# Reordered mixers in layers 3 and 4, and modulation units issued inside the attention of a four-layer fp32 kernel

## The chip, the cores and the metric

The program runs on one core of a Trainium2 chip. The metric is device time in microseconds of one execution, median of several. TensorE (PE) multiplies, VectorE (DVE) and ScalarE (ACT) do elementwise work, GpSimd (POOL) does a little, SyncE (SP) issues the DMAs.

## The reference, cut to what matters

Four transformer-like layers run one after the other on 256 tokens of x and 256 context tokens, 1024 channels, all in float32. Layers 0 and 1 are "first" layers: an attention with grouped keys, a pooling branch and a Fourier branch, one output projection, then a gated feed-forward of width 2816. Layers 2 and 3 ("mixers 3 and 4") are "second" layers: eight heads of differential attention, a convolution branch with 31 taps, both gated and added, an output projection, then a feed-forward of width 4096. Layers 0 and 2 compute both streams (512 columns), layers 1 and 3 compute only x after the keys and values (256 columns).

```python
# each layer: six modulation vectors per stream, from w_ada (1024 x 6144)
mx = silu_c @ w_ada[i] + b_ada[i]        # shift1, scale1, gate1, shift2, scale2, gate2
# second layers
z = a * sigmoid(g)                        # 512 channels of px
z = conv31(z) + b_dw                      # depthwise, along the tokens
y_conv = silu(layernorm(z, ln_g, ln_b)) @ w_conv_out
w = softmax(q1 k1) - lam * softmax(q2 k2) # per head
attn = rmsnorm(w @ v) ; y_attn = attn @ w_attn_out
y = (sigmoid(g_conv) * y_conv + sigmoid(g_attn) * y_attn) @ w_out
x = x + gate1 * y
x = x + gate2 * (relu(modulate(rmsnorm(x)) @ w1) ** 2 @ w2)
```

## The kernel before, in words

Activations lie with channels on the partitions. `plan()` writes one list of steps by hand; `build()` walks that list once per engine, so every engine runs its share of the steps strictly in the list's order, and semaphores tie the engines together. What the list says is the order of everything.

**A weight block** (step `wb`, L134) is a 1024x128 piece of a weight matrix. SP loads it into one of four raw buffers (L980), ACT casts it to `w_hi` (L1157), DVE subtracts to get `w_lo` (L1391), and PE makes 24 matmuls of it, three for each of eight k-tiles (L1036, L1037, L1038), into one of two PSUM banks `out0`, `out1`. Then ACT or DVE evicts the bank. Blocks are split three ahead (AHEAD). The products of the convolution branch have only four k-tiles.

**A modulation unit** (step `ada`, L297) is a 128x1024 piece of `w_ada`. It takes a raw buffer too, all of the same size (512 KB), and PE uses it directly, with a stationary operand of two columns: four matmuls on four column groups of the array, which are eight records in the trace (L1016). Sixteen units fill one bank of modulation vectors, three banks make one layer, 192 units in all. After the sixteenth, DVE transposes the PSUM bank (L1438) and makes the vectors; the first unit of the next bank waits for that. Before, units accumulate in the score bank `sc0` or, in the second layers, in `pt1`.

**The ring of raw buffers.** Weight blocks and units form one stream in the order of the steps (blocks three steps early). SP issues entry r when entry r-4 has been used by PE (a unit) or split by DVE (a block).

**Attention items** (`attend`, L260). One item is 128 queries of one head (or of two paired heads in first layers). On PE: scores S (L1101), transposes T of the previous item's probabilities (L1111), then fill work, PV of the previous item (L1123), then more fill work. DVE takes the maximum (L1596) and normalizes (L1615), ACT makes the exponentials (L1297) and copies the transposes (L1306). Fill work are the projections of the next head, the norms, and in first layers the Fourier and pooling steps. Layer 0 has 16 items, layer 1 has 8, layer 2 has 4 in each of 8 heads, layer 3 has 2 in each of 8.

**Where units stand before.** Bank 0 of layer 0 is the opening. Banks 1 and 2 of layer 0 (32 units) stand between the 13 steps of the head of layer 0 (`spread(head[2:], ada_head)`, L529), which is everything between the first norm and the first score. Layer 1's 48 units: 8 in the second norm of layer 0, 40 spread over the feed-forward of layer 0. Layer 2's 48: 8 and 40 in the same places of layer 1. Layer 3's: 40 in the heads 0 to 3 of layer 2's attention (ten a head, `ada_left`, L717), 8 in its second norm.

**Second layers before** (`layer_second`, L556). First the four pairs of convolution blocks (gate `w_cg`, value `w_ca`), each followed by 8 taps. Then the projections, norms and turns of head 0 with 4 taps after each of their eight functions, and 3 more inside two of them. A tap is one DVE instruction over one of four 128-channel tiles (L1650, and L1647 for the first); there are 124 in a layer. 70 of them stand ahead of the first score of head 0; heads 0 to 4 get the rest. The layer norm of the convolution stands in head 4 (`conv_mean` to `conv_scale`), and its result is written to k-tiles 4 to 7 of `mix_hi`/`mix_lo`, so that the eight gated products (`gated_conv`: a block of `w_gt` and one of `w_conv_out`) have to be through, in head 5, before the output norm of head 4 may be written there. After head 7 come the output norm of head 7 (`out_norm`, L679), eight more gates and eight `w_attn_out` blocks, the merge, and `w_out2`.

Of the kernel before, what the change touches and what calls it, by code (L numbers as in the profile page):

```python
# [19 lines left out]
P = 128  # L20
F32 = mybir.dt.float32
# [75 lines left out]
def plan():  # L97
# [37 lines left out]
    def wb(layer, mat, m, src, k0, nk, n, role, **kw):  # L135
# [3 lines left out]
        s.src_ready = after("act_ready" if src == "act" else "mix_ready")  # L139
# [120 lines left out]
    def attend(items, fills):  # L260
# [4 lines left out]
        for j, item in enumerate(items):  # L265
# [31 lines left out]
    def ada(layer, bank, half, k, psum="sc"):  # L297
        s = step("ada", layer=layer, bank=bank, half=half, k=k, psum=psum)
        s.used = signal("ada_used")
        raw.append(("ada", s))  # L300
        if (half, k) == (0, 0):
            s.sc_free = last.get(("sc", 0)) if psum == "sc" else last.get(("pt", 1))
        if (half, k) == (1, KD - 1):
            s.mods = signal("mods_read")
            last[("sc", 0) if psum == "sc" else ("pt", 1)] = s.mods
            signal("mods_ready")
        return s

# [111 lines left out]
    def layer_first(layer, ada_head=(), gap=(), r=None):  # L420
# [108 lines left out]
        spread(head[2:], ada_head)  # L529
# [6 lines left out]
        for t in range(4):  # L536
# [7 lines left out]
            attend(its, rest)  # L544
        attend_last()
        last["kT", 0] = after("scores_done")
# [6 lines left out]
    def layer_second(layer, ada_head=(), first=(), gap=()):  # L553
# [9 lines left out]
        def conv_taps(count):  # L563

            todo = []
            for _ in range(count):
                t = min(range(len(glu)), key=lambda t: (taps_done[t], t))
                if taps_done[t] == CONV_K:
                    break
                before_it = tap_value[t]  # L570
# [42 lines left out]
        def conv_scale():  # L613
# [6 lines left out]
            finish_mix(s, 4)  # L620
            last["y", 0] = s.mix
# [6 lines left out]
        def product(g, mat, m, k0, nk, role):  # L628
            y = wb(layer, mat, m, "mix", k0, nk, n, role, other=g)
# [35 lines left out]
        def out_norm(h):  # L665
# [11 lines left out]
            def scale():  # L677
# [5 lines left out]
                s.mix_free = None if h < 4 else ("wb_done", state["yconv_end"])  # L683
# [8 lines left out]

        def gated_conv(m):
# [1154 lines left out]
```

## Time and profile before

| | us |
|---|---|
| median of 3 runs | 2612.6 (2610.18 to 2618.47) |
| the profiled execution, its time | 2616.48 |
| the profiled execution, its span | 2614.7 |
| PE busy in it | 2367.3 |
| DVE busy | 1389.5 |
| ACT busy | 1069.2 |
| POOL busy | 33.4 |

The mean granted TensorE clock of that execution is 0.945 of full speed, and 335.87 MB were moved, 128 GB/s on average. Two views are used most. One gives the busy time of each engine in a chosen stretch, with the clock and the DMA rate, one stretch a row. The other lists instructions in order of time, with the idle time ahead of each in square brackets and what ended it. The stretches are cut where the list of steps has its joints: the first score matmul of a head, the first block of a matrix.

### The profile page before, as it was taken

How to read it: one execution, taken by the hardware profiler on the slowest of the kernel's cores; microseconds unless marked ns; L12 is line 12 of the kernel's file. 1: busy time of each engine (PE TensorE's matmuls, PEld its weight loads, DVE VectorE, ACT ScalarE, POOL GpSimd, SP SyncE). 2: the span in 40 equal slices, each digit the busy share in tenths (PEclk: the TensorE clock that was granted, in tenths of full speed). 3: DMA queues.
4: the chain of work that ended last, by engine and by line, in shares of the span. 5: the costliest groups of instructions: out<-in, count | busy, mean ns of one | idle time of the engine just before them, and what ended most of it. 6: DMA issues, size and time to landing. Idle time of an engine off the chain costs nothing.

```text
span 2614.7 us, 34654 instructions
## 1 busy us (share of the span) xinstructions
PE 2367.3 (91%) x13646; PEld 1878.6 (72%) x13646; DVE 1389.5 (53%) x2341; ACT 1069.2 (41%) x1838; POOL 33.4 (1%) x40
## 2 busy tenths in 40 slices
PE   5798899999888999879979899899999788988999
PEld 2466677777666888656658677588888666868999
DVE  4154423333565444788763534544345887555665
ACT  4154421212454333435554532423323546554543
POOL 0300000000010000000000000000000000000000
PEclk8899999999998999889989889899999889989999
DMA  6810434443324777325502122332222211325454
GB/s 260 289 42 33 144 130 154 136 153 121 138 65 161 261 255 242 121 81 194 186 29 86 56 71 88 123 106 97 88 98 101 84 57 53 110 73 178 146 186 145
DMA packets 94880, 335.87 MB, mean 128 GB/s; under 512 B 10624, under 2 KB 12672, under 8 KB 94464
## 3 DMA queue, kind: packets, MB, share of 16 engines
q1 hardware_dynamic: 94720, 333.67, 37.1%
q8 instruction: 109, 1.79, 0.3%
q14 instruction: 51, 0.42, 0.1%
HBM read 332.58 MB, written 1.05 MB: 128 GB/s over the span
## 4 chain that ended last, share of the span: by engine, by line
PE 77%; DVE 10%; ACT 5%; DMA 4%; issue 3%; SPq 0%; ACTq 0%; DVEq 0%
PE out L1036 22%; PE out L1037 21%; PE out L1038 21%; DMA raw<-stream 4%; DVE stage L1650 3%; PE sc L1016 2%; PE pv L1123 2%; PE sc L1101 2%; DVE w_lo L1391 1%; PE pt L1111 1%; PE aux L1046 1%; ACT e_t L1297 1%; ACT w_hi L1157 1%; DVE smax L1596 1%; PE pt L1016 1%
## 5 line engine op out<-in xcount | busy, mean ns | idle before, releaser
L1036 PE MATMUL out<-act_hi,w_lo 128*128 128x512 f32 (+1 forms) x2272 | 813.6, 358 | 57.4 <-DVE act_lo L1550 45.1
L1037 PE MATMUL out<-act_lo,w_hi 128*128 128x512 f32 (+1 forms) x2272 | 793.9, 349 | 0.0
L1038 PE MATMUL out<-act_hi,w_hi 128*128 128x512 f32 (+1 forms) x2272 | 791.4, 348 | 0.0
L1157 ACT CAST w_hi<-raw 128x1024 fp32r<-128x1024 f32 (+2 forms) x444 | 452.5, 1021 | 487.0 <-PE out L1038 434.0
L1391 DVE TENSOR_TENSOR w_lo<-raw,w_hi 128x1024 fp32r<-128x1024 f32 (+2 forms) x444 | 528.0, 1194 | 202.9 <-ACT w_hi L1157 202.5
L1036 PEld LDWEIGHTS out<-act_hi,w_lo 128*128 128x128 f32 x2272 | 442.4, 195 | 149.3 <-issue 86.1
L1038 PEld LDWEIGHTS out<-act_hi,w_hi 128*128 128x128 f32 x2272 | 441.4, 194 | 53.3
L1037 PEld LDWEIGHTS out<-act_lo,w_hi 128*128 128x128 f32 x2272 | 442.7, 195 | 50.4 <-issue 0.5
L1036 PE MATMUL out<-mix_hi,w_lo 128*128 128x256 f32 (+1 forms) x1184 | 403.5, 341 | 3.1 <-DVE mix_lo L1623 1.7
L1037 PE MATMUL out<-mix_lo,w_hi 128*128 128x256 f32 (+1 forms) x1184 | 399.4, 337 | 0.0
L1038 PE MATMUL out<-mix_hi,w_hi 128*128 128x256 f32 (+1 forms) x1184 | 398.9, 337 | 0.0
L1036 PEld LDWEIGHTS out<-mix_hi,w_lo 128*128 128x128 f32 x1184 | 225.8, 191 | 41.0 <-issue 15.5
L1038 PEld LDWEIGHTS out<-mix_hi,w_hi 128*128 128x128 f32 x1184 | 225.9, 191 | 23.4
L1037 PEld LDWEIGHTS out<-mix_lo,w_hi 128*128 128x128 f32 x1184 | 225.9, 191 | 22.5
L1488 DVE SCALAR_TENSOR_TENSOR x<-out,mods,x 128x256 f32<-128x256 f32 x216 | 97.7, 480 | 211.9 <-PE out L1038 211.9
L1463 DVE TENSOR_TENSOR e_t<-e_t,out 128x512 f32<-128x512 f32 (+1 forms) x44 | 24.4, 554 | 260.1 <-PE out L1038 254.3
L1650 DVE SCALAR_TENSOR_TENSOR stage<-stage,vecs 128x512 f32<-128x512 f32 (+1 forms) x240 | 138.5, 613 | 2.3
L1016 PE MATMUL sc<-raw,cv 128*2 128x256 f32 x1152 | 99.1, 430 | 42.7 <-DMA raw<-stream 42.6
L1297 ACT ACTIVATE e_t<-sc,smax,rq 128x512 f32<-128x512 f32 (+1 forms) x144 | 100.7, 705 | 78.6 <-DVE smax L1600 78.5
L1123 PE MATMUL pv<-p_t,v_t 128*64 128x128 f32 (+1 forms) x640 | 88.9, 306 | 28.1 <-ACT p_t L1306 11.9
L1123 PEld LDWEIGHTS pv<-p_t,v_t 128*64 128x64 f32 (+1 forms) x640 | 76.4, 184 | 49.3 <-ACT p_t L1306 37.6
L1470 DVE TENSOR_TENSOR e_t<-e_t,out 128x512 f32<-128x512 f32 (+1 forms) x64 | 35.5, 554 | 137.5 <-ACT e_t L1221 137.4
(160 smaller groups left out, 1732.8 us busy)
## 6 DMA issues: line engine op xcount, KB each, us to landing
raw<-stream SPq DMA_DIRECT2D x604, 512.0 KB, 3.9
raw<-stream SPq DMA_DIRECT2D x16, 384.0 KB, 4.1
raw<-stream SPq DMA_DIRECT2D x16, 256.0 KB, 3.2
x<-xin SPq DMA_DIRECT2D x1, 2048.0 KB, 11.3
consts<-const SPq DMA_DIRECT2D x1, 1344.0 KB, 9.3
x<-ctx SPq DMA_DIRECT2D x1, 1024.0 KB, 5.8
out<-x SPq DMA_DIRECT2D x8, 128.0 KB, 1.7
consts<-const SPq DMA_DIRECT2D x1, 320.0 KB, 11.1
```

The source lines that it names most:

```text
L1016: ins = nc.tensor.matmul(ada_bank[32 * q:32 * q + 2, s.half * NX:(s.half + 1) * NX], cv[:, s.layer // 2, s.k, :], u[:, q], start=(s.k == 0 ...
L1036: nc.tensor.matmul(ps, wl, xh, start=(k == 0), stop=False)
L1037: nc.tensor.matmul(ps, wh, xl, start=False, stop=False)
L1038: ins = nc.tensor.matmul(ps, wh, xh, start=False, stop=(k == s.nk - 1))
L1101: ins = nc.tensor.matmul(scb[h][:, 0:b - a], q_t[rows, it.qslot, it.c0:it.c0 + P], k_t[rows, it.kslot, a:b], start=True, stop=True)
L1123: ins = nc.tensor.matmul(pvb[rows, 0:P], v_t[:, it.vslot, a // P + k, rows], p_t[:, t.slot, k, :], start=(k == 0), stop=(k == nk - 1))
L1157: nc.scalar.copy(w_hi[:, number % HL, 0:n], raw[:, place[number] % RAW, 0:n]).then_inc(S["hi_ready"], 1)
L1297: ins = nc.scalar.activation(e_t[:, 2 * it.e + h, 0:n], scb[h][:, 0:n], ACT.Exp, scale=rq[:, it.qslot, j:j + 1], bias=smax[:, it.e, h:h + ...
L1391: nc.vector.tensor_tensor(w_lo[:, number % HL, 0:n], raw[:, place[number] % RAW, 0:n], w_hi[:, number % HL, 0:n].bitcast(F32), ALU.subtrac ...
L1470: nc.vector.tensor_tensor(e_t[:, 2 + s.hf, 0:s.n], e_t[:, s.sg, 0:s.n], ps, ALU.mult).then_inc(S["out_dve"], 1)
L1488: ins = nc.vector.scalar_tensor_tensor(out=x[:, s.m, cols], in0=ps[:, cols], scalar=mods[:, s.layer, s.gate + s.m, h:h + 1], in1=x[:, s.m, ...
L1650: nc.vector.scalar_tensor_tensor(out=dst, in0=src, scalar=w, in1=dst, op0=ALU.mult, op1=ALU.add)\
```

## The change: what it does

**Units.** In first layers units are no longer fill of the head, but are issued inside `attend`: `pump(n)` takes them from a list `waiting`, and they accumulate in the second output bank `out1`, while the weight blocks of that stretch all use `out0` (`out_slots = 1`). Layer 0's attention gets 48 units, 3 an item (banks 1 and 2 of layer 0, bank 0 of layer 1). The second norm of layer 0 gets 8 and its feed-forward 8 (bank 1 of layer 1). Layer 1's attention gets bank 2 of layer 1, 16 units, 2 an item. Its second norm gets 8, its feed-forward 8 (bank 0 of layer 2). Layer 2's attention gets 72 units, ten a head in heads 0 to 6 and two in head 7.

**Second layers.** The convolution result gets buffers of its own (`conv_hi`, `conv_lo`), and the output norm on ACT has no wait for the gated products any more. Head 0's key and query blocks come first, paired k-tile by k-tile; conv pairs 0 and 1 stand among head 0's other steps, pairs 2 and 3 at the end of heads 0 and 1. 19 taps stand ahead of the first score, the others are spread up to head 6. The layer norm moves from head 4 to head 6 with its mean, centring and squares early in the head. The gated products move from head 5 to head 7, one gate and the product of the gate before it in each group, and the last product stands after the square of the last output norm. `dynamic_dma_scratch_size` is set to 1024.

```diff
@@ wb @@
-        s.out, s.out_free = take("out", 2, rel)
+        s.out, s.out_free = take("out", out_slots, rel)
@@ attend @@
-    def attend(items, fills):
+    def attend(items, fills, units=0):
...
             step("E", item=item)
             part(2 * j)
+            pump(units - units // 2)
             normalize(item)
             if before:
                 values(before)
             part(2 * j + 1)
+            pump(units // 2)
@@ ada @@
+        home = {"sc": ("sc", 0), "pt": ("pt", 1), "out": ("out", 1)}[psum]
...
+    out_slots = 2
+    waiting = []
+
+    def pump(n):
+        for _ in range(min(n, len(waiting))):
+            ada(*waiting.pop(0), psum="out")
@@ layer_first @@
-        spread(head[2:], ada_head)
+        for f in head[2:]:
+            f()
+        waiting.extend(inside)
+        out_slots = 1
...
-            attend(its, rest)
+            attend(its, rest, units)
         attend_last()
+        pump(len(waiting))
+        out_slots = 2
@@ layer_second @@
-        for t in range(4):
+        def conv_gate(t):
             g = w("w_cg", t, n, "sg", func=ACT.Sigmoid)
             g.qg, g.qg_free = take("sgl", 2, None)
-            a = w("w_ca", t, n, "glu", other=g, free=last.get(("cz", 0)))
-            if t == 0:
-                together(g, a)
-            last["sgl", g.qg] = a.rel
-            glu.append(a)
-            conv_taps(8)
+            glu.append(g)
+        def conv_value(t):
+            g = glu[t]
+            glu[t] = w("w_ca", t, n, "glu", other=g, free=last.get(("cz", 0)))
+            last["sgl", g.qg] = glu[t].rel
+        def conv_pair(t):
+            conv_gate(t)
+            conv_value(t)
...
         def gated_conv(m):
             def go():
-                product(gate(m), "w_conv_out", m, 4, 4, "yconv")
-                state["yconv_end"] = len(blocks)
+                if m:
+                    product(conv_gates[m - 1], "w_conv_out", m - 1, "conv", 4, "yconv")
+                if m < KD:
+                    conv_gates.append(gate(m))
             return go
...
-        for f in head_work(0):
-            f()
-            conv_taps(4)
+        q_block, k_block, q_norm, q_done, v_block, k_norm, k_done, v_turn = head_work(0)
+        k_block()
+        q_block()
+        together(held["k", 0], held["q", 0])
+        q_norm()
+        v_block()
+        q_done()
+        k_norm()
+        conv_pair(0)
+        k_done()
+        v_turn()
+        conv_taps(8)
+        conv_pair(1)
+        conv_taps(8)
...
+            if h < 2:
+                if both:
+                    groups[6].append(lambda h=h: conv_gate(2 + h))
+                    groups[7].append(lambda h=h: conv_value(2 + h))
+                else:
+                    groups[3].append(lambda h=h: conv_pair(2 + h))
-            if both and h == 4:
-                groups[4].append(conv_mean)
-                groups[5].append(conv_centre)
-                groups[6].append(conv_squares)
+            if both and h == 6:
+                groups[1].append(conv_mean)
+                groups[2].insert(0, conv_centre)
+                groups[3].append(conv_squares)
                 groups[7] += [conv_rstd, conv_scale]
...
-            if h == 5:
-                if both:
-                    for m in range(KD):
-                        groups[4 + m // 4].append(gated_conv(m))
...
+            if h == 7:
+                per = KD // len(groups)
+                for m in range(KD):
+                    groups[m // per].append(gated_conv(m))
...
-                slots = (4 - h) * len(groups) - j + (4 if both else 1)
+                slots = (6 - h) * len(groups) - j + 1
...
         square()
+        gated_conv(KD)()
         total()
@@ program @@
-    layer_first(0, [lambda a=a: ada(*a) for a in ada_list(0, [1, 2])], ada_list(1)[:8], r)
-    ffn(0, NT, ada_list(1)[8:], NT)
-    layer_first(1, gap=ada_list(2)[:8])
-    ffn(1, NX, ada_list(2)[8:], NT)
-    layer_second(2, ada_list(3)[:40], gap=ada_list(3)[40:])
+    layer_first(0, ada_list(0, [1, 2]) + ada_list(1, [0]), 3, ada_list(1, [1])[:8], r)
+    ffn(0, NT, ada_list(1, [1])[8:], NT)
+    layer_first(1, ada_list(1, [2]), 2, ada_list(2, [0])[:8])
+    ffn(1, NX, ada_list(2, [0])[8:], NT)
+    layer_second(2, ada_list(2, [1, 2]) + ada_list(3)[:40], gap=ada_list(3)[40:])
@@ tensor @@
+                            xh = hi[:, s.k0 + k, 0:g.n]
+                            xl = lo[:, s.k0 + k, 0:g.n]
@@ scalar, ox @@
-                    wait(act, s.mix_free)
@@ vector @@
+            nc.vector.memset(outb[1][:, :], 0.0)
             nc.vector.memset(scb[0][:, :], 0.0).then_inc(S["bank_zero"], 1)
```

## Rows read from the trace of the kernel before

**Rows 1.** The page, busy time of each engine over the span.

```profile
PE 2367.3 (91%) x13646; PEld 1878.6 (72%) x13646; DVE 1389.5 (53%) x2341; ACT 1069.2 (41%) x1838; POOL 33.4 (1%) x40
```

**Rows 2.** Stretches: length, busy of PE, PEld, DVE, ACT, POOL; clock, DMA share, GB/s.

```profile
319.60:650.30 330.70, 330.70 (x1618) 253.28 (x1618) 106.16 (x134) 78.29 (x96) 0.00 (x0) 1.00 0.41 141
833.00:1055.60 222.60, 220.77 (x1904) 197.32 (x1904) 110.11 (x148) 86.94 (x120) 0.00 (x0) 1.00 0.71 247
1700.00:2000.00 300.00, 300.00 (x1325) 248.51 (x1324) 127.99 (x170) 87.90 (x116) 0.00 (x0) 1.00 0.29 99
2440.00:2600.00 160.00, 158.89 (x1318) 158.07 (x1317) 99.92 (x140) 73.79 (x111) 0.00 (x0) 1.00 0.55 181
```

**Rows 3.** Stretches: head and attention of layer 0, then of layer 1.

```profile
64.00:129.50 65.50, 50.25 (x371) 26.47 (x370) 13.11 (x20) 11.38 (x20) 20.22 (x22) 0.86 0.81 282
129.50:234.00 104.50, 92.90 (x530) 59.44 (x530) 54.55 (x148) 52.88 (x144) 0.00 (x0) 0.94 0.09 31
711.00:729.00 18.00, 15.06 (x112) 13.79 (x112) 10.54 (x14) 11.27 (x22) 5.67 (x6) 1.00 0.78 271
729.00:793.60 64.60, 53.72 (x380) 37.99 (x380) 37.32 (x90) 33.41 (x85) 7.29 (x9) 0.98 0.12 39
```

**Rows 4.** Units alone (L1016) in heads 0 to 3 of layer 2: PE, PEld.

```profile
1160.00:1300.00 140.00, 22.88 (x304) 4.86 (x304) 0.97 0.52 185
```

**Rows 5.** PE in order of time: start, length, records, idle before and its releaser.

```profile
129.75 2.08 PE L1101 MATMUL sc<-k_t,q_t 64*128 64x512 f32 x4 [0.91 <-DVE p_t L1438]
...
1151.45 2.08 PE L1101 MATMUL sc<-k_t,q_t 64*128 64x512 f32 x4 [6.44 <-DVE k_t L1570]
...
2095.78 2.08 PE L1101 MATMUL sc<-k_t,q_t 64*128 64x512 f32 x4 [5.02 <-DVE k_t L1570]
```

**Rows 6.** Stretches of layer 2, cut at the first scores of heads.

```profile
1116.50:1151.50 35.00, 20.25 (x93) 16.09 (x91) 34.30 (x54) 11.15 (x19) 0.00 (x0) 0.82 0.19 61
1151.50:1190.50 39.00, 36.57 (x216) 23.74 (x216) 31.21 (x61) 16.54 (x37) 0.00 (x0) 0.90 0.39 133
1190.50:1226.60 36.10, 34.52 (x228) 22.62 (x224) 29.95 (x61) 20.31 (x44) 0.00 (x0) 1.00 0.55 196
1302.00:1344.50 42.50, 34.65 (x154) 24.07 (x150) 29.51 (x59) 22.33 (x48) 0.00 (x0) 0.90 0.15 50
1344.50:1383.50 39.00, 30.45 (x121) 22.23 (x121) 20.54 (x42) 24.57 (x46) 0.00 (x0) 0.79 0.07 21
1489.60:1517.00 27.40, 18.79 (x62) 10.56 (x61) 15.32 (x38) 12.29 (x29) 0.00 (x0) 0.56 0.00 0
1151.50:1518.10 366.60, 328.52 (x1675) 229.43 (x1675) 233.73 (x462) 185.78 (x375) 0.00 (x0) 0.91 0.30 105
```

**Rows 7.** Stretches of layer 3: ahead of head 0; the eight heads.

```profile
2070.40:2095.80 25.40, 16.88 (x88) 13.83 (x88) 24.94 (x55) 9.99 (x18) 0.00 (x0) 0.91 0.30 104
2095.80:2338.80 243.00, 211.19 (x1167) 169.28 (x1167) 166.34 (x345) 140.16 (x286) 0.00 (x0) 0.93 0.21 72
```

**Rows 8.** Taps alone (L1650), DVE busy in head 1 of layers 2 and 3.

```profile
1190.50:1226.60 36.10, 10.04 (x14) 1.00 0.55 196
2119.60:2144.80 25.20, 6.04 (x14) 1.00 0.18 63
```

**Rows 9.** ACT in order of time: table load, exponential, split, a query's eviction.

```profile
1357.36 1.28 ACT L1140 ACT_TABLE_LOAD   x1 [2.12 <-DVE smax L1600]
1358.66 0.78 ACT L1297 ACTIVATE e_t<-sc,smax,rq 128x512 f32<-128x512 f32 x1
...
1360.18 1.03 ACT L1157 CAST w_hi<-raw 128x1024 fp32r<-128x1024 f32 x1
1361.12 0.60 ACT L1187 ACTIVATE sq<-out 128x512 f32<-128x512 f32 x1
1361.61 0.48 ACT L1189 ACTIVATE qg<-out,vecs 128x256 f32<-128x256 f32 x1
```

**Rows 10.** The page, DMA issues: size and median time to landing.

```profile
raw<-stream SPq DMA_DIRECT2D x604, 512.0 KB, 3.9
```

More of the change, by code:

```diff
@@ L138, in wb @@
         blocks.append((mat, m, kw.get("wk0", 0), nk))
-        s.src_ready = after("act_ready" if src == "act" else "mix_ready")
+        s.src_ready = after({"act": "act_ready", "mix": "mix_ready", "conv": "conv_ready"}[src])
         release = {"q": "out_act", "v": "out_act", "pool": "out_act", "sg": "out_act", "sig": "out_act"}.get(role, "out_dve")
         rel = signal(release)
-        s.out, s.out_free = take("out", 2, rel)
+        s.out, s.out_free = take("out", out_slots, rel)
         s.rel = rel
@@ L300, in ada @@
         raw.append(("ada", s))
+        home = {"sc": ("sc", 0), "pt": ("pt", 1), "out": ("out", 1)}[psum]
         if (half, k) == (0, 0):
-            s.sc_free = last.get(("sc", 0)) if psum == "sc" else last.get(("pt", 1))
+            s.sc_free = last.get(home)
         if (half, k) == (1, KD - 1):
-            s.mods = signal("mods_read")
-            last[("sc", 0) if psum == "sc" else ("pt", 1)] = s.mods
+            s.mods = last[home] = signal("mods_read")
             signal("mods_ready")
         return s
+    out_slots = 2
[3 more added lines that the diff above has]
+            ada(*waiting.pop(0), psum="out")
     def ada_list(layer, banks=range(ADA_BANKS)):
@@ L418, in q_items, with layer_first @@
         return out
-    def layer_first(layer, ada_head=(), gap=(), r=None):
+    def layer_first(layer, inside, units, gap, r=None):
+        nonlocal out_slots
         both = layer == 0
@@ L566, in conv_taps @@
             for _ in range(count):
-                t = min(range(len(glu)), key=lambda t: (taps_done[t], t))
-                if taps_done[t] == CONV_K:
+                left = [t for t in range(len(glu)) if glu[t].role == "glu" and taps_done[t] < CONV_K]
+                if not left:
                     break
+                t = min(left, key=lambda t: (taps_done[t], t))
                 before_it = tap_value[t]
@@ L619, in conv_scale @@
             signal("ln_h", 4)
-            finish_mix(s, 4)
-            last["y", 0] = s.mix
+            last["y", 0] = signal("conv_ready", 4)
         def gate(tile):
@@ L626, in gate, with product @@
             return g
-        def product(g, mat, m, k0, nk, role):
-            y = wb(layer, mat, m, "mix", k0, nk, n, role, other=g)
+        def product(g, mat, m, src, nk, role):
+            y = wb(layer, mat, m, src, 0, nk, n, role, other=g)
             if role == "yattn":
@@ L762, in layer_second @@
                 gates.append(gate(KD + m))
-            y = product(gates[m], "w_attn_out", m, 0, KD, "yattn")
+            y = product(gates[m], "w_attn_out", m, "mix", KD, "yattn")
             y.by_k = m == 0
@@ L848, in build @@
         mix_lo = sb("mix_lo", [P, KD, NT], F32R)
+        conv_hi = sb("conv_hi", [P, 4, NT], F32R)
+        conv_lo = sb("conv_lo", [P, 4, NT], F32R)
         raw = sb("raw", [P, RAW, UNIT])
@@ L991, in _ @@
         def _(pe):
-            seen = {"act": 0, "mix": 0}
+            seen = {"act": 0, "mix": 0, "conv": 0}
             def need(src, name, value):
@@ L1019, in _ @@
                 elif s.kind == "wb" and (s.mate is None or s.number < s.mate.number):
-                    hi, lo = (act_hi, act_lo) if s.src == "act" else (mix_hi, mix_lo)
+                    hi, lo = {"act": (act_hi, act_lo), "mix": (mix_hi, mix_lo), "conv": (conv_hi, conv_lo)}[s.src]
                     group = [s] if s.mate is None else [s, s.mate]
@@ L1329, in _ @@
                         link(nc.scalar.activation(b, b, ACT.Silu, scale=col(s.layer, "ln_g", t), bias=col(s.layer, "ln_b", t)))
-                        nc.scalar.copy(mix_hi[:, 4 + t, 0:s.n], b).then_inc(S["ln_h"], 1)
+                        nc.scalar.copy(conv_hi[:, t, 0:s.n], b).then_inc(S["ln_h"], 1)
                 elif s.kind == "merge":
```

32 lines of the change are left out of this document (14 added, 18 removed).

## The prediction

> **What bounds the kernel now.** I began with the busy times on the page [rows 1]: PE is busy 91% of the span, DVE 53%, ACT 41%. So what can be won is 247 us of PE idle time, the time that PE runs at the lower of its two clock levels (mean grant 0.945), and nothing else: the change removes no block and no unit. Next came the stretches. In the feed-forward PE is busy throughout at full clock, with one record every 300/1325 = 0.226 us at 512 columns and 160/1318 = 0.121 us at 256 [rows 2], so a block takes 24 times that, 5.43 and 2.91 us. Everything put there costs its full price. The opposite is true in the heads: layer 2's eight heads have 366.6 - 328.5 = 38 us idle at clock 0.91, layer 3's 32 us at 0.93, the attentions of layers 0 and 1 12 and 11 us [rows 3, 6, 7]. Then PE in order of time at the first scores: in layers 2 and 3 they wait 6.4 and 5.0 us for `k_t` from DVE [rows 5], and just there DVE is busy 34.3 of 35.0 and 24.9 of 25.4 us, PE only 20.3 and 16.9 [rows 6, 7]: 70 taps stand ahead. Last, the head of layer 0 moves 282 GB/s over 65.5 us [rows 3], which is 36 entries of the ring (32 units, 4 blocks) at 1.8 us each: DMA bounds it, PE idles 15 us.
>
> **Feed-forwards, 32 units fewer in each.** The clean stretch holds 34 units, 272 of 1618 records. The other 1346 take 305 us, so 26 us are left for 34 units: 0.76 us each [rows 2]. 32 of them are 24.3 us, twice: -48.6. Nothing covers a unit there, PE being 100% busy, and nothing else becomes late: DVE has 106 us of work in 331, and layer 1's feed-forward, which moves 247 GB/s, only gets lighter. Bounds -22 to -26 each.
>
> **Layer 0.** Without units, the stretch that now goes from 64.0 to the first score at 129.75 [rows 3, 5] holds four blocks (21.7 us) and the short steps. Layer 1 has the same head without units: 18.0 us with four blocks of 2.91, so 6.4 us of short steps, some 2 of them already past at 64.0, plus 1 for wider columns [rows 3]. That makes 27, and the first score comes at 91, 38.5 us earlier. Then 48 units go into 16 items. In layer 2 they already stand among items: 38 units take 22.9 us of PE, 0.60 each [rows 4], so 48 cost 28.8. They fall ahead of PV and of the next scores, where this attention idles 11.6 us; I let them fill 8. The first unit of a new bank must wait until DVE has transposed the old one, three times, 1 us each I suppose, behind a normalization; DVE, half idle there (54.6 of 104.5), loses nothing that I count. The four blocks now share one bank, but scores stand between them, and ACT's eviction (0.60 + 0.48 + 0.48) is through: 0. DMA needs 52 entries in some 127 us, 2.4 us each against 1.8. Attention +23, layer 0 together -16. Ends: -21 (all idle filled, no turn-over cost) and +1 (0.76 each, nothing filled, the turn-overs).
>
> **Layer 1.** 16 units in 8 items: 9.6 us, of 10.9 us idle some 3.5 filled since most of it stands elsewhere, 1 for waits: +7 (0 to +12).
>
> **Layer 2.** Up to the first score: the first pair ends as now, at 1082, paced by the norm. Then the query sum waits for a new thing. ACT, behind it in the list, must evict the keys (0.60 + 0.68), split a block (1.03) and evict the queries (1.56) [rows 9]: some 4 us, while the value block is queued behind that wait on PE. Then 0.9 + value block 5.4 + key norm 1.3 + transposes 0.4 + four conv blocks 21.7 = 1116 against 1151.45: 35 us earlier. DVE has 51 taps fewer there, at 10.04/14 = 0.72 us [rows 8]. Inside the heads +21.7 for the four conv blocks that moved there and +19.2 for 32 units. What goes: head 1 shows what a warm head takes, 36.1 - 1.6 idle - 6 for ten units = 28.5 [rows 6]. Head 4 takes 42.5 without units, and the first part of head 5 39.0 instead of 24.5 (4 us of a warm head come behind it): the convolution's norm loses 28. With its first three steps early in head 6, units around it, and a gate block ahead of the first PV of head 7, I keep 15 (-13). Head 7 up to the output norm takes 27.4 us at clock 0.56 for 11 us of warm work; with eight gates and seven products among its items nearly all of that goes (-13; the eighth product covers the square of the last output norm). Heads 0, 1 and 6 get filler at their transposes (-4.5), and slow starts of heads 5 and 6 go (-5.5). Sum: 366.6 + 40.9 - 36 = 371.5. Layer 2 -35 + 5 = -30. Ends: -45 and -10.
>
> **Layer 3.** The same with 256 columns: pair to 2049, 4 + 0.9 + 5.4 + 1.3 + 0.4 + 11.6 = 2072 against 2095.8, 24 earlier. In the heads +11.6 for four blocks, -8 for the convolution's norm, -8 at the end, +2 for taps (18 a head instead of 14, at 6.04/14 = 0.43 us [rows 8]). Together -26 (-36 to -10).
>
> **At nothing.** The added clearing of an output bank (a 128x512 clearing beside a first matmul that waits for DMA), `conv_hi` in place of `mix_hi`, the removed ACT wait (its gated products are now far behind), the smaller scratch: the queue that carries all weights issues through SP, and even a rate a tenth lower than 282 GB/s would leave each stretch after the change below it. POOL's windows of layer 0 now run beside the attention that needs them only in its last tiles.
>
> **Sum.** -48.6 - 16 + 7 - 30 - 26 = -113.6. The profiled execution took 2616.5 us, so 2503; it lies 3.9 above the median of the runs shown, against which the forecast is 2499, in round numbers 2500.
>
> **Rivals.**
>
> *The idle time moves instead of going.* Layer 2's head 1 has DVE busy 30.0 of 36.1 us with 14 taps [rows 6, 8]. Afterwards heads 0 and 1 have 22, heads 2 to 5 14 to 17, and 16 more stand between the keys of head 0 and its first maximum. If DVE's order decides, heads 0 to 5 lose some 3 us each in layer 2 and 2 in layer 3, and the norm in head 6 keeps all its 28: 30 + 13 less won, 2540. For it: scores now wait on ACT and DVE there. Against: 30 us fit in 36.
>
> *ACT changes tables too often.* Sigmoid gates now stand singly among exponentials, and each change is an ACT_TABLE_LOAD of 1.28 us that stands between the maximum and the exponential [rows 9]. I count 4 more gates apart from each other in heads 0 and 1, 5 more in head 7 of both layers, so 18 loads with the way back: 23 us if all are on the path, 2523. Against: a gate block covers a load. The exponential starts 0.02 us after the load's end. The Trainium skill (ScalarE: Activation LUTs, section "What ACT_TABLE_LOAD costs") says that a drain of about 1.38 us comes on top of the 1.28 and advises to do all of one set before switching. By that page it would be 48 us and 2548; the trace has the load's length but not the drain.
>
> *More is filled than I allow.* All of the idle time in the attentions of layers 0 and 1 and the whole of the convolution norm's loss: another 30, 2470.
>
> *The ring starves the attention (slower).* A unit in the attention has its DMA issued only when the entry four before it is used; PE takes two units at once, and 512 KB need 3.9 us to land [rows 10]. If PE stood the landing at each of the 32 places in layer 0 and 16 in layer 1, that is 187 us, and 2690. It turns slower than before at 113.6/48 = 2.4 us a place. Against: at 185 GB/s in layer 2's heads 38 units among 140 us leave PE busy, and layer 0 asks for about 225 of the 282 GB/s shown.
>
> **How the numbers follow.** Forecast 0.62 (its own range 2485 to 2520), idle moves 0.18, more filled 0.12, tables 0.05, ring 0.03. The range 2470 to 2545 takes in all but the ring and the far ends. This kernel's runs tell 0.3%, 8 us, from no change. Faster 0.96, same 0.01, slower 0.03.
>
> **What would show it.** First scores near 91 in layer 0 and 1116 - 58 = 1058 in layer 2; feed-forwards of 0 and 1 24 us shorter each; a unit in the attention at 0.6 us with little idle ahead from DMA; head 7 at full clock. Wrong: PE waits for `raw` in layer 0, the exponential waits of layer 2 grow, or PE idles more than 150 us in all.

## The result, and the profile after

The changed kernel takes 2536.8 us (median of 4 runs, 2535.2 to 2538.3), the kernel before took 2611.4 beside it (2606.2 to 2618.5): ratio 0.9713, 95% interval 0.9688 to 0.9737. That is 75 us less where the forecast was 113 less. The time lies inside the range 2470 to 2545, but nearer to the rival "the idle time moves instead of going" (2540) than to the forecast (2500), and the layers show that this is more than a coincidence of numbers.

On the page, PE is busy 41 us less than in [rows 1], and idle 210 us instead of 247. The 13646 records are the same in both, while the mean granted clock rose from 0.945 to 0.958. So more than half of the 78 us between the two profiled executions is PE's own work getting shorter, and not idle time that went. The 210 us are also above the 150 that the forecast had named as a sign of being wrong.

```profile
PE 2326.3 (92%) x13646; PEld 1867.4 (74%) x13646; DVE 1394.4 (55%) x2342; ACT 1091.6 (43%) x1856; POOL 35.2 (1%) x40
raw<-stream SPq DMA_DIRECT2D x604, 512.0 KB, 3.4
```

The stretches after, columns as in [rows 2], cut at the same steps of the list. In order: heads 0, 6 and 7 of layer 2, the last head of layer 3, the eight heads of layer 2, the eight heads of layer 3, the attentions of layers 0 and 1.

```profile
1051.10:1109.30 58.20, 48.59 (x267) 33.75 (x266) 43.73 (x76) 21.59 (x42) 0.00 (x0) 0.85 0.40 136
1309.90:1361.80 51.90, 41.99 (x232) 25.66 (x228) 30.79 (x66) 22.83 (x49) 0.00 (x0) 0.87 0.38 127
1361.80:1447.60 85.80, 80.16 (x370) 62.19 (x367) 40.22 (x69) 52.85 (x77) 0.00 (x0) 0.96 0.32 99
2203.50:2262.80 59.30, 46.78 (x338) 43.77 (x337) 31.68 (x57) 38.23 (x62) 0.00 (x0) 0.88 0.34 111
1051.10:1447.60 396.50, 358.81 (x2027) 245.18 (x2027) 278.87 (x528) 205.62 (x392) 0.00 (x0) 0.94 0.43 146
2003.10:2262.80 259.70, 221.66 (x1264) 181.18 (x1263) 198.25 (x409) 154.35 (x300) 0.00 (x0) 0.94 0.24 78
88.00:204.40 116.40, 110.83 (x914) 61.84 (x915) 60.53 (x156) 53.06 (x144) 8.97 (x10) 1.00 0.68 235
675.50:748.00 72.50, 63.05 (x508) 39.27 (x509) 39.41 (x93) 33.61 (x85) 7.85 (x9) 0.98 0.46 157
```

Cut that way, the whole difference of the two profiled executions (2614.7 and 2536.5 of span) falls into these parts:

| stage | before | after | difference | forecast |
|---|---|---|---|---|
| layer 0: opening | 48.5 | 47.3 | -1.2 | |
| layer 0: first key block to first score | 81.3 | 40.7 | -40.6 | -38.5 |
| layer 0: attention | 104.3 | 116.4 | +12.1 | +23 |
| feed-forward of layer 0 | 402.1 | 378.9 | -23.2 | -24.3 |
| layer 1: attention | 64.5 | 72.5 | +8.0 | +7 |
| layer 1: output projection and norm | 39.3 | 36.7 | -2.6 | |
| feed-forward of layer 1 | 235.8 | 215.9 | -19.9 | -24.3 |
| layer 2: up to the first score | 82.7 | 50.4 | -32.3 | -35 |
| **layer 2: eight heads** | 366.6 | 396.5 | **+29.9** | **+5** |
| layer 3: up to the first score | 59.0 | 37.7 | -21.3 | -24 |
| **layer 3: eight heads** | 243.0 | 259.7 | **+16.7** | **-2.4** |

What is left (ends of layers 2 and 3, the other parts) changes by -4. So everything outside the heads of the second layers came within 5 us of the forecast or better, and 44 us were lost in those heads. The idle time of PE in layer 2's heads is the same as before, 396.5 - 358.8 = 37.7 against 38.1 in [rows 6], in layer 3's 38.0 against 31.8 in [rows 7], although 41 and 12 us of work, at the forecast's prices, were put in. (A feed-forward in the table ends at the first block of the next layer, its norm included.)

The two first scores that were the clearest targets, and the first of layer 0:

```profile
88.00 1.13 PE L1142 MATMUL sc<-k_t,q_t 64*128 64x512 f32 x4 [1.44 <-DVE q_t L1567]
...
1051.13 1.13 PE L1142 MATMUL sc<-k_t,q_t 64*128 64x512 f32 x4
...
2003.06 1.13 PE L1142 MATMUL sc<-k_t,q_t 64*128 64x512 f32 x4
```

The 6.44 and 5.02 us behind `k_t` of [rows 5] are gone, and these scores run at the high clock (1.13 us against 2.08 for the same four). What replaced the waits stands in the list of PE's waits (us in total, times, longest), first in head 0 of layer 2, then in head 6, then in its head 7, then in head 7 of layer 3:

```profile
PE sc L1142 <- ACT e_t L1338: 6.4, 1, 6.4
PE pt L1152 <- DVE e_t L1656: 3.2, 2, 2.9
...
PE aux L1170 <- DVE stage L1699: 3.9, 1, 3.9
PE aux L1096 <- DVE stage L1704: 3.5, 1, 3.5
...
PE pv L1164 <- DVE o_t L1668: 4.4, 1, 4.4
...
PE out L1077 <- ACT qg L1255: 5.7, 2, 3.9
PE out L1077 <- DVE conv_lo L1723: 4.7, 1, 4.7
```

The first one is read by following DVE in order of time: the exponential is late because its maximum is late, and the maximum (L1637) stands behind eight taps, a first one of a tile at 1054.75 us and the seven of this row (L1691).

```profile
1055.33 5.47 DVE L1691 SCALAR_TENSOR_TENSOR stage<-stage,vecs 128x512 f32<-128x512 f32 x7
1060.72 1.28 DVE L1637 TENSOR_REDUCE smax<-sc 128x1 f32<-128x512 f32 x2
```

### The profile page after: what moved, and what is told of

Its sections match the earlier page's. It is cut to its first block, busy times and chain, and to the rows that moved or that the text cites. A ratio compares the mean times of both kernels' runs of the same rounds, so it can differ in the third digit from the quotient of the medians.

```text
span 2536.5 us, 34665 instructions
## 1 busy us (share of the span) xinstructions
PE 2326.3 (92%) x13646; PEld 1867.4 (74%) x13646; DVE 1394.4 (55%) x2342; ACT 1091.6 (43%) x1856; POOL 35.2 (1%) x40
## 3 DMA queue, kind: packets, MB, share of 16 engines
q1 hardware_dynamic: 94720, 333.67, 39.3%
## 4 chain that ended last, share of the span: by engine, by line
PE 77%; DVE 11%; ACT 6%; issue 3%; DMA 2%; SPq 0%; ACTq 0%; DVEq 0%
PE out L1077 22%; PE out L1078 22%; PE out L1079 22%; DMA raw<-stream 2%; DVE stage L1691 2%; PE pv L1164 2%; PE sc L1142 1%; DVE w_lo L1431 1%; PE pt L1152 1%; ACT w_hi L1198 1%; ACT e_t L1338 1%; PE aux L1087 1%; DVE smax L1637 1%; PE pt L1057 1%; PE out L1057 1%
## 5 line engine op out<-in xcount | busy, mean ns | idle before, releaser
L1077 PE MATMUL out<-mix_hi,w_lo 128*128 128x512 f32 (+1 forms) x1120 | 378.4, 338 | 4.3 <-DVE mix_lo L1664 1.7
L1078 PE MATMUL out<-mix_lo,w_hi 128*128 128x512 f32 (+1 forms) x1120 | 377.0, 337 | 0.0
L1079 PE MATMUL out<-mix_hi,w_hi 128*128 128x512 f32 (+1 forms) x1120 | 376.9, 337 | 0.0
L1077 PEld LDWEIGHTS out<-mix_hi,w_lo 128*128 128x128 f32 x1120 | 212.9, 190 | 30.7 <-issue 4.7
L1079 PEld LDWEIGHTS out<-mix_hi,w_hi 128*128 128x128 f32 x1120 | 212.9, 190 | 22.0
L1078 PEld LDWEIGHTS out<-mix_lo,w_hi 128*128 128x128 f32 x1120 | 212.8, 190 | 21.9
L1691 DVE SCALAR_TENSOR_TENSOR stage<-stage,vecs 128x512 f32<-128x512 f32 (+1 forms) x240 | 141.8, 615 | 3.1
L1637 DVE TENSOR_REDUCE smax<-sc 128x1 f32<-128x512 f32 (+1 forms) x144 | 79.6, 595 | 39.1 <-PE sc L1142 39.0
L1347 ACT COPY p_t<-pt 128x512 f32<-128x512 f32 (+1 forms) x96 | 46.9, 515 | 114.2 <-PE pt L1152 114.2
L1262 ACT ACTIVATE e_t<-out 128x512 f32<-128x512 f32 (+1 forms) x64 | 31.5, 493 | 146.0 <-PE out L1079 146.0
## 6 DMA issues: line engine op xcount, KB each, us to landing
consts<-const SPq DMA_DIRECT2D x1, 320.0 KB, 11.3
```

The lines of the kernel that those rows point to most:

```text
L1077: nc.tensor.matmul(ps, wl, xh, start=(k == 0), stop=False)
L1078: nc.tensor.matmul(ps, wh, xl, start=False, stop=False)
L1079: ins = nc.tensor.matmul(ps, wh, xh, start=False, stop=(k == s.nk - 1))
L1347: nc.scalar.copy(p_t[:, t.slot, 0:n // P, :], ptb[t.bank][:, 0:n].rearrange("p (t n) -> p t n", n=P))\
L1637: ins = nc.vector.reduce_max(smax[:, it.e, h:h + 1], scb[h][:, 0:n], AX_X)
L1691: nc.vector.scalar_tensor_tensor(out=dst, in0=src, scalar=w, in1=dst, op0=ALU.mult, op1=ALU.add)\
```

## The experiments

Every experiment starts from the changed kernel, and every time is compared with the kernel before on the same chip. "Change" below is the 0.9713 above.

### Which half of the change brings what

The units alone, with the second layers in their old order:

```diff
-        k_block()
-        q_block()
-        together(held["k", 0], held["q", 0])
...            (conv pairs first, layer norm in head 4, products in head 5: as before)
+        for f in head_work(0):
+            f()
+            conv_taps(4)
```

> The units move as in the change (48 into the attention of layer 0, 16 into that of layer 1, 72 into the heads of layer 2), while layers 2 and 3 keep their old order. If the parts add up: layers 0 and 1 as in the changed kernel, -66 us by the traces of before and after (head and attention of layer 0 -28, its feed-forward -23, attention of layer 1 +8, feed-forward -20, small joints -3), and 32 more units in layer 2's heads 4 to 7 at +5 to +19 us: 2611 - 66 + 12 = 2557, between 2550 and 2565. Theory 'idle time moves': the 32 units in the old order fill the idle time of the convolution's norm in heads 4 and 5, so close to +5. Rival 'a unit in a head costs its 0.6 us whatever stands there': +19, 2564.

Measured 2553.4, ratio 0.9776 (0.9763 to 0.979). The heads of layer 2 take 370.3 us, 3.7 more than before with 32 more units in them. Three numbers make up that small price: the units (L1032 there, L1016 before) are busy 19.7 us more, PE's idle time falls by 5.6, from 38.1 to 32.5, and the old work takes 10.4 less at a granted clock of 0.94 instead of 0.91:

```profile
1084.10:1454.40 370.30, 337.79 (x1930) 227.20 (x1931) 235.57 (x468) 185.68 (x375) 0.00 (x0) 0.94 0.44 150
```

The new order alone, with the units where they were. The convolution's products read k-tiles 0 to 3 of the attention's result instead of the convolution's, so that the values differ and the work and its waits don't.

```diff
-    layer_first(0, ada_list(0, [1, 2]) + ada_list(1, [0]), 3, ada_list(1, [1])[:8], r)
+    layer_first(0, [lambda a=a: ada(*a) for a in ada_list(0, [1, 2])], ada_list(1)[:8], r)
```

> The new order of layers 2 and 3, with every unit where it was before. By the traces the start of layers 2 and 3 wins 32 + 21 us, less 22 + 12 for the conv blocks moved behind the first score, 19 us; the rest, what the heads win by the new order, is open. Theory 'the heads win nothing' (PE's idle time in the eight heads of layer 2 was 38.1 us before and is 37.7 after, in layer 3 31.8 and 38.0): 2611 - 19 = 2592. Rival, my prediction's terms without the units (-49 and -26): 2540.

Measured 2591.1, ratio 0.992 (0.9906 to 0.9934), which is what the theory "the heads win nothing" said (2592). The heads of layer 2 take 385.3, 18.7 more, for the 21.7 us of convolution blocks that moved in, and are idle 43.8 us, more than before:

```profile
1117.70:1503.00 385.30, 341.53 (x1772) 243.65 (x1771) 276.19 (x523) 205.58 (x392) 0.00 (x0) 0.94 0.31 107
```

The product of the two ratios is 0.9698, inside the interval of the change: the halves add. The units bring three quarters of the gain. The same 32 units that cost 3.7 us in the old order cost 396.5 - 385.3 = 11.2 in the new one. It is not that they found less idle time: they filled 6.1 us of it (43.8 to 37.7), about as much as in the old order. But the clock, 0.94 without them, stayed at 0.94, and the old work got only some 3 us shorter.

### The taps ahead of the first maximum

```diff
         conv_pair(1)
-        conv_taps(8)
```

> The changed kernel with the 8 taps taken out that stand between conv pair 1 and the first scores of head 0 (the spreading over the heads takes them up). Theory 'DVE's order': the first maximum of head 0 starts 5.5 us earlier in layer 2 and 3.5 in layer 3, the 6.4 us wait of the second scores and the slow clock after it (k block 7.64 instead of 5.44 us) go: head 0 from 58.2 to about 49 us, in all -7 to -12 us, 2526. Rival 'the stall is ACT's' (table load and exponentials behind the evictions): head 0 stays within 2 us of 58.2, and the time within 0.1%.

Measured 2533.9, ratio 0.9701 (0.9687 to 0.9714). Head 0 of layer 2 goes from 58.2 to 51.3 us, and the wait for the exponential from 6.4 to 0.4:

```profile
PE pt L1151 <- DVE e_t L1655: 3.9, 2, 3.7
PE sc L1141 <- ACT e_t L1337: 0.4, 1, 0.4
```

The stall in head 0 is as the theory has it. The whole time does not show it: its interval overlaps that of the change. In layer 3 the same edit wins 1.6 us in head 0 and loses 4.6 in the later heads, where the taps stand now; so little of it is left in the time.

### The norm of the convolution

Its square root and scaling moved from the end of head 6 of layer 2 into the middle:

```diff
-                groups[3].append(conv_squares)
-                groups[7] += [conv_rstd, conv_scale]
+                groups[3] += [conv_squares, conv_rstd, conv_scale]
```

> The changed kernel with the reciprocal root and the scaling of the convolution's norm of layer 2 right behind its squares, in group 3 of head 6 instead of group 7. Theory 'the chain of the norm at the joint of heads 6 and 7 is on the path': the 4.35 us wait of PV at the start of head 7 and the slow matmuls behind it go, -6 to -8 us in layer 2, 2530. Rival 'the chain costs the same wherever it stands' (about 8 DVE and 8 ACT passes of 0.6 to 0.8 us that the attention of that moment has to wait for): the wait turns up in the middle of head 6, time unchanged within 2 us.

Measured 2537.7, ratio 0.9724 (0.9709 to 0.9738): nothing won. Heads 6 and 7 of layer 2 then are

```profile
1303.70:1368.70 65.00, 44.63 (x232) 26.97 (x228) 36.41 (x73) 32.79 (x62) 0.00 (x0) 0.79 0.31 100
1368.70:1446.40 77.70, 76.99 (x371) 60.34 (x367) 34.37 (x62) 43.27 (x63) 0.00 (x0) 1.00 0.35 111
```

Head 7 is clean, with 0.7 us idle, and 8.1 us shorter (77.7 for 85.8), which is what the chain costs it in the changed kernel. Head 6 has lost 13 more: the wait has only moved, now as one of 11.3 us of a unit for DVE:

```profile
PE pt L1056 <- DVE stage L1478: 11.3, 1, 11.3
```

The statistics left out altogether (in layer 2 as below, in layer 3 likewise):

```diff
-                groups[1].append(conv_mean)
-                groups[2].insert(0, conv_centre)
-                groups[3].append(conv_squares)
-                groups[7] += [conv_rstd, conv_scale]
+                groups[7] += [conv_scale]
```

> The changed kernel without mean, centring, squares and reciprocal root of the convolution's norm in both layers (they are left out; scaling, silu and the split of the result stay). Theory 'the norm is still on the path': by PE's idle time and slow matmuls heads 6 and 7 of layer 2 lose 27 us against a warm head, of which the statistics are what stands in head 6: -14 us in layer 2 (51.9 to 38) and -6 in layer 3, 2517. Rival 'head 6 is long because of its units and taps': within 3 us of the changed kernel.

Measured 2507.1, ratio 0.9596 (0.9578 to 0.9615). Head 6 of layer 2 drops from 51.9 to 37.6 us, that of layer 3 from 32.4 to 23.5. This is the price of the statistics with the square root: 14.3 and 8.9 us, for two short sums on PE and 7 us of DVE (23.81 busy instead of 30.79 in head 6 of layer 2):

```profile
1303.70:1341.30 37.60, 34.82 (x230) 22.48 (x226) 23.81 (x53) 20.02 (x44) 0.00 (x0) 1.00 0.51 174
```

The theory was right in its two heads (38 expected in layer 2) and too low in total (2517): by the ratios the time fell by 30.6 us, of which these two heads are 23.2. The rest is spread over other stages, 2.2 of it in head 7 of layer 2, and is not explained.

The scaling chain put behind the first gate of head 7, and the products two gates late. In layer 3 the eight gates are also spread differently over the four groups, 1, 2, 2 and 3 instead of two in each, so the three edits are not told apart there:

```diff
-                if m:
-                    product(conv_gates[m - 1], "w_conv_out", m - 1, "conv", 4, "yconv")
+                if m > 1:
+                    product(conv_gates[m - 2], "w_conv_out", m - 2, "conv", 4, "yconv")
...
+                if m == 0:
+                    conv_scale()
```

> The changed kernel with the scaling chain of the convolution's norm taken from the end of head 6 to behind the first gate of head 7 in both layers, and every product one gate later (two gates ahead of the first product). Theory 'the chain needs PE work that waits for nothing beside it': the 4.35 us wait of PV and the slow matmuls behind it in layer 2, and the 4.7 and 3.9 us waits for conv_lo and the gate in layer 3 go: -6 and -8 us, 2523. Rival 'the chain costs the same anywhere': the waits turn up behind the first two gates, within 2 us.

Measured 2531.8, ratio 0.9686 (0.9671 to 0.97). Head 7 of layer 3 goes from 59.3 to 54.5, that of layer 2 only from 85.8 to 84.5. In layer 3 the gate's eviction is waited for 1.8 us instead of 5.7 in all, but `conv_lo` is now waited for 5.9. ACT in order of time shows why. A table load for the gate (from 2207.12 us), the gate's eviction, a table load for the chain (from 2208.91) and then the chain's four activations and four casts follow each other without a gap until 2214.0, and the product starts at 2214.66. The theory (2523) was too high in its gain, the rival's waits did turn up, and the whole time, with an interval that overlaps that of the change, does not decide.

The statistics kept, but moved by a group in layer 2, so that the key block of the head stands between the adds and the matmul that needs them:

```diff
-                groups[1].append(conv_mean)
-                groups[2].insert(0, conv_centre)
-                groups[3].append(conv_squares)
+                groups[2].append(conv_mean)
+                groups[3].insert(0, conv_centre)
+                groups[4].append(conv_squares)
```

> The change with only the three statistics steps of the convolution's norm moved inside head 6 of layer 2: mean at the end of group 2, centring at the start of group 3, squares in group 4, so that the head's key block stands between the adds of DVE and the matmul that waits for them, and the four centring passes hold the auxiliary bank while a block runs. In layer 3 mean and centring stand at the start of group 1. Theory, the two waits of head 6 (3.9 us for the adds, 3.5 us of the query sum for the auxiliary bank) are a matter of place: 6 to 8 us less in layer 2, 2 to 3 in layer 3, 2528 (0.968). Rival, the norm costs the same wherever it stands, as in the run with the chain moved into head 6: within 2 us of 2537.

Measured 2530.3, ratio 0.9681 (0.9657 to 0.9705). Head 6 of layer 2 and its longest waits:

```profile
1305.20:1345.10 39.90, 36.80 (x232) 22.96 (x228) 30.75 (x66) 22.73 (x50) 0.00 (x0) 1.00 0.50 167
```

```profile
PE pt L1056 <- DVE stage L1478: 1.2, 1, 1.2
PE pt L1151 <- DVE e_t L1655: 1.1, 2, 0.8
```

12.0 us less in that head, more than either theory said, and for about the same 232 matmuls, 66 DVE and 50 ACT instructions. The 3.9 and 3.5 us waits are gone: idle time falls from 9.9 to 3.1. The other 5.2 us are PE's own work, 41.99 against 36.80 us busy, at a granted clock of 0.87 against 1.00. So a wait of a few microseconds cost nearly twice its length: 12.0 us for 6.8 of idle time, the rest being work at a lower granted clock. Layer 3, where mean and centring moved forward, won nothing (its head 6 takes 33.8 instead of 32.4), and head 7 of layer 2 takes 87.4 instead of 85.8. So less arrives in the whole time: by the ratios 8 us, and the two intervals overlap. The rival, 2535 or more, lies outside the interval (2522 to 2534).

In the changed kernel these are the two places in order of time. The first matmul needs the last of three adds, which DVE makes right before. The second needs the auxiliary bank, and the four centring passes that read it (L1704) stand on DVE behind the maximum of the next item.

```profile
1322.83 2.07 PE L1170 MATMUL aux<-stage,consts 128*128 128x512 f32 x2 [3.89 <-DVE stage L1699]
...
1331.92 1.84 PE L1096 MATMUL aux<-consts,sq 128*128 128x2 f32 x8 [3.49 <-DVE stage L1704]
```

```profile
1322.08 0.69 DVE L1699 TENSOR_TENSOR stage<-stage 128x512 f32<-128x512 f32 x1
...
1327.90 1.29 DVE L1637 TENSOR_REDUCE smax<-sc 128x1 f32<-128x512 f32 x2 [4.93 <-PE sc L1142]
...
1329.30 2.48 DVE L1704 SCALAR_TENSOR_TENSOR stage<-aux,stage 128x512 f32<-128x512 f32 x4
```

### Table loads

```diff
-            g = w("w_cg", t, n, "sg", func=ACT.Sigmoid)
+            g = w("w_cg", t, n, "sg", func=ACT.Identity)
...
-                        nc.scalar.activation(qg[:, s.qg, 0:s.n], ps, ACT.Sigmoid, bias=col(s.layer, "b_gate", s.tile))\
+                        nc.scalar.activation(qg[:, s.qg, 0:s.n], ps, ACT.Identity, bias=col(s.layer, "b_gate", s.tile))\
```

> The changed kernel with the identity in place of the sigmoid in all gates of layers 2 and 3 (so the gates are left out), which needs no table of its own: some 36 of the 42 table loads of 1.28 us go. Theory 'loads are covered by blocks': most stand while PE multiplies a block, so at most -6 us, 2531. Rival 'table loads are on the path' (18 more of them than before the change, 23 us): -20 us or more, under 2517. The drain of 1.38 us a load that the Trainium skill tells of (ScalarE: Activation LUTs, section on what a table load costs) would make it -45.

Measured 2521.3, ratio 0.9646 (0.9631 to 0.966). The heads of the two layers:

```profile
1051.50:1439.50 388.00, 354.79 (x2028) 243.26 (x2027) 278.67 (x528) 186.62 (x377) 0.00 (x0) 0.96 0.43 150
1992.60:2247.10 254.50, 219.86 (x1264) 179.05 (x1263) 197.57 (x409) 141.34 (x290) 0.00 (x0) 0.95 0.25 79
```

8.5 and 5.2 us less, and the time lies between the two theories (2531 and 2517). The changed kernel has 42 loads of 1283 ns where the kernel before has 24, so the 18 of the rival were counted right. Here 10 are left, so 2536.8 - 2521.3 = 15.5 us (17.5 by the ratios) by 32 is 0.5 us each. By that price the 18 added ones cost some 9 us, not the rival's 23; this is an estimate, since no run takes out just those.

### DVE's total

16 of the 31 taps of each tile:

```diff
-                left = [t for t in range(len(glu)) if glu[t].role == "glu" and taps_done[t] < CONV_K]
+                left = [t for t in range(len(glu)) if glu[t].role == "glu" and taps_done[t] < 16]
```

> The changed kernel with 16 of the 31 taps (the others are left out): 60 DVE instructions fewer in each of layers 2 and 3, 43 and 26 us of DVE time. Theory 'DVE's order decides in head 0 and nowhere else': head 0 of layer 2 falls by 2 to 7 us since fewer taps stand ahead of its maxima later in the head, heads 1 to 5 stay within 1 us each, in all -5 to -10 us, 2530. Rival 'the heads are DVE-bound by the spread taps': heads 0 to 5 lose a third of the saved DVE time, -20 us or more, under 2517.

Measured 2509.3, ratio 0.9608 (0.959 to 0.9626). The heads of layers 2 and 3:

```profile
1047.50:1428.90 381.40, 352.74 (x2028) 242.67 (x2027) 239.50 (x468) 205.06 (x392) 0.00 (x0) 0.96 0.45 152
1981.60:2227.80 246.20, 217.01 (x1263) 177.24 (x1263) 173.48 (x349) 154.26 (x300) 0.00 (x0) 0.96 0.25 82
```

Each lost 60 DVE instructions, 39.4 and 24.8 us of DVE, and came out 15.1 and 13.5 us shorter. PE stood idle 28.7 and 29.2 us in them instead of 37.7 and 38.0. My theory said 5 to 10 in all; the rival, that spread taps delay maxima and normalizations everywhere, was right. In layer 3's heads 3 to 5 idle time falls from 3.7, 3.2 and 2.8 to 1.2 us each.

### All together

Two of the edits, then all three, beside each other on one chip. (The tap edit is here in layer 2 alone.)

```diff
-        conv_taps(8)
+        conv_taps(0 if both else 8)
```

> The scaling chain of the convolution's norm behind the first gate of head 7 (alone it gave 0.9686, 5 us less than the change), and in layer 2 no eight taps between the second convolution pair and the first maximum (alone 0.9701, 3 us less, 7 in head 0 of layer 2, of which layer 3 lost some again; here the taps of layer 3 stay as in the change). If the two costs are separate stalls, they add: head 0 of layer 2 51 us, head 7 of layer 3 54.5, together 5 + 5, 2526 (ratio 0.967). Rival, DVE's total in the heads decides: the taps taken out of head 0 come back in heads 1 to 5, and the time stays at 2531 (0.969).

> All three together: scaling chain behind the first gate of head 7, no eight taps ahead of the first maximum of layer 2, statistics moved in head 6. If all are separate stalls: the sum of the two runs beside it, 2536.8 - 10 - 9 = 2518 (0.964). If DVE's total decides, no better than the better of the two, 2526.

Measured 2528.3, ratio 0.9671 (0.9647 to 0.9696), and 2516.1, ratio 0.9626 (0.9604 to 0.9649). The first interval holds both of its expectations (0.967 and 0.969), so by the time alone it decides nothing. The second came out as expected if the stalls are separate (2518), and better than the rival's 2526. It is the best version of the study, 0.9% below the changed kernel and clear of its interval. The heads of layer 2 in it:

```profile
1050.80:1429.00 378.20, 350.28 (x2028) 241.09 (x2027) 278.41 (x529) 205.66 (x392) 0.00 (x0) 0.97 0.44 153
```

378.2 instead of 396.5 us with the same instructions, 18.3 won: 6.9 in head 0, 11.1 in head 6, 1.5 in head 7, and 1.3 given back in heads 1 to 5. In layer 3 only 2.1 us were won (257.6 for 259.7). The stalls of layer 2 are separate, and they add; DVE's total (278.4 us busy as ever) does not forbid it.

## Why the prediction was right or wrong

**Feed-forwards.** Layer 0's -23.2 for -24.3: a unit among fp32 blocks costs 0.73 us. Layer 1's came 4.4 short. At its end three blocks wait 1.5 us in all for the residual's eviction by DVE, where before units stood and no such wait shows. "Nothing else becomes late" missed that. It is not the whole: idle time rose by 1.9 us, and PE's busy time fell by only 21.6 for 24.3.

**Layer 0.** The head came out at 40.6 less for 38.5, the first score at 88.0 for 91. The attention was priced too high, +12.1 for +23 (the terms as written, 28.8 - 8 + 3, give 23.8). The 48 units take 26.9 us of PE, 0.56 each for 0.60, and 6.0 us of idle time were filled for 8. What I left out is the clock: 0.94 in [rows 3], 1.00 now, with 5.6 us idle in it for 11.6. PE's busy time rose by 17.9 us, 0.37 a unit, so the old work got 9 us shorter.

```profile
88.00:204.40 116.40, 26.90 (x384) 6.54 (x384) 1.00 0.68 235
```

The ring starved nothing: 235 GB/s went through against about 225 forecast, and PE waited once for a raw buffer, for 0.4 us.

**Layer 1.** +8.0 for +7: right.

**Up to the first scores of layers 2 and 3.** -32.3 for -35 and -21.3 for -24: right, with the first score of layer 2 at 1051 for 1058 and that of layer 3 with no wait before it. The wait of the query sum that I priced at 4 us is there and took 2.8 us in layer 2 (L1096 behind ACT's `q_t`) and 2.6 in layer 3.

**The heads of layers 2 and 3** are where it failed, in two steps. One was put at nothing or nearly so: the DVE work that moved into the heads (below). The other was worked out, on the convolution's norm: "With its first three steps early in head 6, units around it, and a gate block ahead of the first PV of head 7, I keep 15 (-13)", and in layer 3 "-8 for the convolution's norm". By the runs head 6 pays 14.3 and 8.9 us for the statistics alone. That is what head 4 lost before: 14.0 in layer 2 (42.5 for a warm 28.5), 8.6 in layer 3 (32.9 for the 24.3 of the head ahead of it). Head 7 still waits for the chain as well: 4.4 us ahead of PV in layer 2, whose first product then runs at the low clock (0.63 us a record for 0.39), and 4.7 for `conv_lo` in layer 3. In layer 2 that chain is worth 8.1 us, by the run that moved it out of head 7. So the norm costs 14.3 + 8.1 = 22.4 us there, where I kept 15 of 28, and in layer 3 nothing of the statistics' loss was won. What I had argued from was that units stand around the steps. But the waits of head 6 are 3.9 and 3.5 us and a unit is 0.56; what covers such a wait is a block, and no block stood there. Moving three steps by a group brought 12.0 us in that head, 10.4 with head 7.

The rest of the 44 us. These costs overlap, and do not add up to it:
- Head 0 of layer 2, 6.9 for eight of the 16 taps between its keys and its first maximum. The rival named them, the forecast did not price them. The fillers (-4.5) do not show either: head 1 is idle 2.5 us (48.10 - 45.55), where it was 1.6.
- Taps in the other heads: "+2 for taps" in layer 3 was mis-sized. By the run with half the taps, DVE work spread over the heads costs 0.4 us (layer 2) and 0.5 us (layer 3) for each microsecond of it. The change moved 45.1 and 31.9 us of DVE work into the heads (278.87 for 233.73, 198.25 for 166.34). At these prices that is some 17 us in each layer, head 0's stall included: an estimate, against 0 and 2 in the forecast. If it holds it is the larger miss: the norm's is 7.4 us in layer 2 and at most 8 in layer 3.
- The added table loads, some 9, priced by me at nothing in the forecast.
- Head 7 of layer 3, 59.3. With four groups for eight gates and seven products, evictions behind a table load (3.9 us ahead of one block) are waited for; 4.8 went with the products a gate later and the gates spread anew. The rest stays open: with all three edits that head still is idle 10.2 of 55.4 us.

**The rivals.** "The idle time moves" had the right mechanism and 2540 the right size. In its places it was half right: the norm kept its loss and head 0 lost 7, but heads 2 to 5 of layer 2 took only 37.1 to 39.9 us. Tables: counted right, priced more than twice too high. "More is filled" was not true: 6.0 of 11.6 us in layer 0 and 1.4 of 10.9 in layer 1, both less than I allowed. What made layer 0 cheap was the clock. The ring: wrong, see above. The size 2540 is in part luck, since it holds neither the 9 us of table loads nor head 7 of layer 3. The 0.18 for the first was too little: a body with DVE busy 30.0 of 36.1 us in one head [rows 6] was the warning, and I met it with "30 us fit in 36", which is about sums and not about who stands behind whom.

On the page of the Trainium skill named there (ScalarE: Activation LUTs, "What ACT_TABLE_LOAD costs"): the load's length agrees, 1283 ns in each of the loads after, and here the cast ahead of it ends, and the activation behind it starts, within 0.02 us of it. So no drain of 1.38 us shows.

```profile
1377.34 0.61 ACT L1198 CAST w_hi<-raw 128x512 fp32r<-128x512 f32 x1
1377.96 1.28 ACT L1255 ACT_TABLE_LOAD   x1
1379.26 0.69 ACT L1255 ACTIVATE qg<-out,vecs 128x512 f32<-128x512 f32 x1
```

The 48 us by that rule did not come, some 9 did. The advice to finish one set before switching, which stands in the page's section "Table sets: the hidden batching unit", holds for this kernel all the same, at 0.5 us a load.

## What to carry to other kernels

Idle time that ends behind a chain over two engines is not filled by putting work somewhere in the same stage: list each hand-over of the chain, and put between the two sides a piece of work as long as the chain's step (here a block of 5.4 us, not a unit of 0.56). When a stage is filled up, ask of each instruction of the second engine which short, urgent one queues behind it, above all a maximum or a normalization; the sum of its busy time says nothing of that. Price a removed stall at more than its length where the clock is below 1.00 behind it, and look at small waits that removed work had covered.

## What the runs showed that I had not expected

- Stalls and the clock: head 6 of layer 2 did the same work in 41.99 us of PE at a grant of 0.87 with 9.9 us idle, in 36.80 at 1.00 with 3.1 idle, and in 44.63 at 0.79 with 20.4 idle (232 records each time).
- The same works in the other direction: 48 units into layer 0's attention raised its clock from 0.94 to 1.00, and they cost 12 us net, a quarter of a microsecond each. In the old order of layer 2, 32 units did it again, from 0.91 to 0.94, for 3.7 us net.
- The placing of three short steps, ten DVE instructions and two sums on PE, was worth 12 us in one head (10.4 with the head behind it), nearly as much as leaving out half the taps of the layer (15).
